# A hybrid decoder layer on one core: other homes for rows and small arrays, row numbers behind up, first weights in three parts

## What is computed

```python
proj = rmsnorm(x) @ w_in                  # 1024 x 7168, eight parts
m = sigmoid(ga) * conv_branch(cv, cg) + sigmoid(gb) * hgrn2_branch(q, f, v, og)
x = x + m @ w_out
# hierarchical experts: top-1 of 4 groups, top-2 of its 8 experts
h = rmsnorm(x)
for e in range(32):
    a = silu(h @ w_expert_gate[e]) * (h @ w_expert_up[e])
    out += combine[:, e:e+1] * (a @ w_expert_down[e])
y = rmsnorm(x + out)                      # and the new states of both branches
```

## Time and profile before

| | us |
|---|---|
| median of 3 runs (802.21 to 802.62) | 802.27 |
| the profiled execution | 801.55 |
| its span | 799.8 |
| TensorE busy | 776.8 |
| mean granted TensorE clock, share of full | 0.996 |
| HBM read | 259.14 MB |

### The profile page before, as it was taken

One profiled execution on the slowest core, in us unless ns is written; L12 is line 12 of the kernel. 1 busy time (PEld: TensorE's weight loads), 2 busy tenths in 40 slices (PEclk: granted clock), 3 DMA queues, 4 the chain that ended last, 5 costly groups with the idle time before them and its releaser, 6 DMA issues.

```text
span 799.8 us, 10083 instructions
## 1 busy us (share of the span) xinstructions
PE 776.8 (97%) x4132; PEld 440.1 (55%) x4132; DVE 236.5 (30%) x540; ACT 172.6 (22%) x313; POOL 96.6 (12%) x130
## 2 busy tenths in 40 slices
PE   8999999999999999999999999999998999999996
PEld 7888888888888887853333333333323333323332
DVE  4099859482550321441201110011101101101102
ACT  3104333657544101410011001110010010011101
POOL 5200064523300000001101000001000000000001
PEclk9999999999999999999999999999999999999999
DMA  9845586668749975589999999999999999999994
GB/s 331 246 153 187 164 236 201 187 211 183 264 147 360 399 265 206 188 325 433 423 429 416 427 429 428 429 425 429 427 426 429 429 427 427 429 426 420 421 410 156
DMA packets 76374, 266.82 MB, mean 334 GB/s; under 512 B 5726, under 2 KB 37706, under 8 KB 63775
## 3 DMA queue, kind: packets, MB, share of 16 engines
q1 hardware_dynamic: 74402, 263.05, 84.4%
q10 hardware_dynamic: 1461, 1.45, 0.6%
q0 software_dynamic: 464, 1.64, 0.5%
HBM read 259.14 MB, written 7.47 MB: 333 GB/s over the span
## 4 chain that ended last, share of the span: by engine, by line
PE 76%; DMA 19%; DVE 1%; issue 1%; POOL 1%; SPq 0%; ACT 0%; DVEq 0%
PE bank L1642 23%; PE bank L2040 22%; DMA slots<-in_w_expert_gate_dram 10%; PE bank L2078 8%; PE bank L1915 7%; PE bank L2086 5%; DMA x_early<-in_w_expert_gate_dram 5%; DMA slot<-in_w_expert_up_dram 3%; PE bank L1862 2%; PE bank L1752 1%; DMA slots<-in_w_in_dram 1%; PE bank L2004 1%; PE bank L1674 1%; PE bank L2067 1%; PE bank L2092 1%
## 5 line engine op out<-in xcount | busy, mean ns | idle before, releaser
L1642 PE MATMUL bank<-hT,slots 128*128 128x264 f32 x832 | 189.6, 387 | 0.0
L2040 PE MATMUL bank<-slots,hT 128*64 128x512 f32 x624 | 181.8, 601 | 5.6 <-DMA slots<-in_w_expert_gate_dram 5.0
L1642 PEld LDWEIGHTS bank<-hT,slots 128*128 128x128 f32 x832 | 156.6, 190 | 26.8 <-issue 0.6
L2040 PEld LDWEIGHTS bank<-slots,hT 128*64 128x64 f32 x624 | 55.8, 138 | 107.3 <-issue 94.2
L1501 DVE TENSOR_TENSOR x_early<-x_early,bank 128x512 f32<-128x512 f32 x16 | 11.0, 688 | 344.5 <-PE bank L2040 344.5
L2078 PE MATMUL bank<-slots,wrep 128*64 128x512 f32 x304 | 85.1, 595 | 0.1
L2040 PE MATMUL bank<-slot,hT 128*64 128x512 f32 x208 | 81.9, 595 | 2.4 <-DMA slot<-in_w_expert_gate_dram 1.7
L2086 PE MATMUL bank<-hT,diag 128*128 128x512 f32 x128 | 64.4, 615 | 0.2 <-ACT hT L1068 0.2
L796 POOL COPY hT<-x_early 128x512 f32 x30 | 17.6, 614 | 369.5 <-PE bank L2040 285.5
L2078 PEld LDWEIGHTS bank<-slots,wrep 128*64 128x64 f32 x304 | 26.1, 137 | 45.6 <-issue 40.1
L1226 DVE SCALAR_TENSOR_TENSOR slot<-slot,rows_buf 128x256 f32<-128x256 f32 x120 | 49.4, 488 | 0.0
(11 more groups left out here) (313 smaller groups left out, 747.7 us busy)
## 6 DMA issues: line engine op xcount, KB each, us to landing
slots<-in_w_expert_gate_dram SPq DMA_DIRECT2D x15, 2048.0 KB, 26.3
slots<-in_w_expert_up_dram SPq DMA_DIRECT2D x15, 2048.0 KB, 31.2
slots<-in_w_expert_down_dram SPq DMA_DIRECT2D x15, 2048.0 KB, 33.6
slots<-in_w_in_dram SPq DMA_DIRECT2D x13, 2048.0 KB, 10.2
slots<-in_w_expert_gate_dram SPq DMA_DIRECT2D x10, 1024.0 KB, 26.4
slot<-in_w_expert_gate_dram SPq DMA_DIRECT2D x5, 2048.0 KB, 25.4
slot<-in_w_expert_up_dram SPq DMA_DIRECT2D x5, 2048.0 KB, 26.2
slot<-in_w_expert_down_dram SPq DMA_DIRECT2D x5, 2048.0 KB, 29.5
```

Of the source, the lines that this page charges most:

```text
L1642: last = mm(out, w[:, a, t * P:(t + 1) * P], (hT if c else xgain)[:, a, :], start=(a == 0), stop=(a == KT - 1))
L2040: last = mm(out[sl, :], xe[:, a, sl], expert_view(p, kind, e, a // 2)[:, a % 2, :], start=(a == 0), stop=(a == KT - 1))
```

## The change

1. *Homes.* The three tiles of `xrow` move: to `ytok` (the upper part of hT), to `rows_buf` and to `early[2D:3D]`. The small arrays move to the place of `act` and to free columns of `xall`. Halves 17 and 19 are free earlier: load 19 is issued ahead of slot 5, load 17 after the squares are summed. The rows are written to memory tile by tile, and ACT waits for that before it writes `ytok` in pair 0.
2. *Row numbers behind up.* `row_numbers` stands behind up(0), the list's copy behind `swiglu(0)` on DVE, and turn(0) waits for it.
3. *First weights in three parts*: 512 KB, 512 KB and 1 MB. The load of `norm_mix_g` moves from SyncE's queue to ACT's, and one of four fillers goes.
4. *Row products of a pair in one block*: all four of `combine_prompt(p - 1)` stand between gate(p) and up(p) (in pair 15 in the middle of gate), and `m_rows` goes.
5. *Whole slots in pair 14*: all its weights come as whole slots and no longer by halves.

```diff
+        small_homes = [act, *(xall[:, a, 2 * P:LISTED] for a in (0, 5, 6, 7))]
+        xrow = [ytok, rows_buf[:, 0:D], early[:, 2 * D:3 * D]]
+        xrow_by = [x.rearrange("p (a q) -> p a q", a=KT) for x in xrow]
...
         def by_halves(p, kind):
-            return p == PAIRS - 2 or (p, kind) in ((1, 2), (PAIRS - 1, 0))
+            return (p, kind) in ((1, 2), (PAIRS - 1, 0))
...
-            sp.dma_start(vecr[0:KT, :], ins["norm_mix_g"][0].rearrange("(r c) -> r c", c=P)).then_inc(gain_in, 16)
...
-            sp.dma_start(slot3(0)[:, 0:KT // 2, :], stream[0][0][:, 0:KT // 2, :]).then_inc(first_in, 16)
+            sp.dma_start(slot3(0)[:, 0:2, :], stream[0][0][:, 0:2, :]).then_inc(first_in, 16)
+            sp.dma_start(slot3(0)[:, 2:KT // 2, :], stream[0][0][:, 2:KT // 2, :]).then_inc(second_in, 16)
...
             load(WO + 1)
+            load_half(NR - 1)
...
             load_half(16)
+            sp.wait_ge(f_sum, KT - 1)
+            load_half(17)
             sp.wait_ge(misc.ready, misc.written(("ht", 5)))
             sp.wait_ge(x_kept, 1)
             load_half(18)
-            sp.wait_ge(row_made, 6)
-            sp.dma_start(tok_rows[0:SEQ, :].rearrange("(t p) d -> p t d", p=P), xrow[:, 0:2, :]).then_inc(rows_kept, 16)
+            for t in range(2):
+                sp.wait_ge(row_made, 2 * t + 4)
+                sp.dma_start(tok_rows[t * P:(t + 1) * P, :], xrow[t]).then_inc(rows_kept, 16)
...
-            sp.wait_ge(rows_kept, 32)
+            load_half(NR)
+            sp.wait_ge(rows_kept, 48)
             sp.wait_ge(m_gathered, 2)
-            load_half(19)
-            sp.wait_ge(smalls_done, 1)
-            load_half(17)
-            load_half(NR)
...
+            se.dma_start(vecr[0:KT, :], ins["norm_mix_g"][0].rearrange("(r c) -> r c", c=P)).then_inc(gain_in, 16)
...
+                if p == 0:
+                    se.wait_ge(rows_kept, 48)
                 if p:
                     se.wait_ge(m_comb, p)
-                    se.wait_ge(m_rows, p)
...
-            dve.wait_ge(m_numbers, 1)
-            dve.tensor_copy(list_at[:, 1:], numbers).then_inc(list_ready, 1)
...
             for p in range(PAIRS):
                 swiglu(p)
+                if p == 0:
+                    dve.wait_ge(m_numbers, 1)
+                    dve.tensor_copy(list_at[:, 1:], numbers).then_inc(list_ready, 1)
...
-            keep_busy(4)
+            keep_busy(3)
...
                 for a in range(4 * half, 4 * half + 4):
+                    if a == 2:
+                        pe.wait_ge(second_in, 16)
...
-                hidden(p, 0, bank[GATE], m_gate, (lambda: combine_prompt(p - 1, 2)) if p == PAIRS - 1 else None)
+                hidden(p, 0, bank[GATE], m_gate, (lambda: combine_prompt(p - 1)) if p == PAIRS - 1 else None)
...
                 else:
-                    pe.wait_ge(smalls_done, 1)
+                    pe.wait_ge(list_ready, 1)
...
                 gate(p)
+                if 1 < p < PAIRS - 1:
+                    combine_prompt(p - 1)
+                up(p)
                 if p == 0:
                     row_numbers()
-                if 1 < p < PAIRS - 1:
-                    combine_prompt(p - 1, 2 if late_rows(p - 1) else 4)
-                up(p)
                 if p:
                     combine_samples(p - 1)
-                if p and late_rows(p - 1):
-                    to_rows(p - 1, 1, 0)
                 turn(p)
-                if p and late_rows(p - 1):
-                    to_rows(p - 1, 1, 1).then_inc(m_rows, 1)
```

More of the change, by code:

```diff
@@ L190, in hybrid_layer @@
         PAIR_ORDER = (1, 0, 2, 3)
-        xrow = early[:, 0:3 * D].rearrange("p (t d) -> p t d", t=3)
-        xrow_by = early[:, 0:3 * D].rearrange("p (t a q) -> p t a q", t=3, a=KT)
         xall = early[:, 3 * D:3 * D + KT * COLS].rearrange("p (a c) -> p a c", a=KT)
@@ L216, in hybrid_layer @@
         wc_zero = dflat[:, T:T + QUART]
-        o = 0
+        taken = [0] * len(small_homes)
         def flat(n):
[L220 to L223, removed]
+            i = next(i for i, home in enumerate(small_homes) if taken[i] + n <= home.shape[1])
+            taken[i] += n
+            return small_homes[i][:, taken[i] - n:taken[i]]
         def small(n):
@@ L276, in hybrid_layer @@
         x_turned, x_gained, x_copied = sem("x_turned"), sem("x_gained"), sem("x_copied")
-        first_in, gain_in = sem("first_in"), sem("gain_in")
+        first_in, second_in, gain_in = sem("first_in"), sem("second_in"), sem("gain_in")
         x_squared, rms_ready, diag_ready = sem("x_squared"), sem("rms_ready"), sem("diag_ready")
@@ L599, in _ @@
             load_half(18)
-            sp.wait_ge(row_made, 6)
-            sp.dma_start(tok_rows[0:SEQ, :].rearrange("(t p) d -> p t d", p=P), xrow[:, 0:2, :]).then_inc(rows_kept, 16)
+            for t in range(2):
+                sp.wait_ge(row_made, 2 * t + 4)
+                sp.dma_start(tok_rows[t * P:(t + 1) * P, :], xrow[t]).then_inc(rows_kept, 16)
             sp.wait_ge(*misc.read(("ht", 5)))
-            sp.dma_start(tok_rows[SEQ:T, :], xrow[0:NB, 2, :]).then_inc(rows_kept, 16)
+            sp.dma_start(tok_rows[SEQ:T, :], xrow[2][0:NB, :]).then_inc(rows_kept, 16)
             sp.wait_ge(quad_ready, 1)
@@ L780, in fetch_rows @@
                 pool.wait_ge(m_gathered, 2 * b)
-                pool.indirect_dma_start(xrow[0:m, 2, :], None, tok_rows[:, :],
+                pool.indirect_dma_start(xrow[2][0:m, :], None, tok_rows[:, :],
                                         bass.IndirectOffsetOnAxis(ap=list_at[0:m, b:b + 1], axis=0)).then_inc(row_in, 16)
@@ L786, in _ @@
             pool.wait_ge(*made("xend"))
-            pool.wait_ge(rows_kept, 32)
+            pool.wait_ge(rows_kept, 48)
             pool.wait_ge(list_ready, 1)
@@ L1033, in _ @@
                 se.wait_ge(y_seated, i + 1)
-                se.activation(xrow_by[:, t, :, SLOTS * half:SLOTS * half + SLOTS],
+                se.activation(xrow_by[t][:, :, SLOTS * half:SLOTS * half + SLOTS],
                               bank[Y_BANKS[t][half]][:, :].rearrange("p (q a) -> p a q", a=KT), ACT.Copy,
@@ L1038, in _ @@
                 se.wait_ge(misc.ready, misc.written(("ht", 4 + half)))
-                se.activation(xrow_by[0:NB, 2, :, SLOTS * half:SLOTS * half + SLOTS],
+                se.activation(xrow_by[2][0:NB, :, SLOTS * half:SLOTS * half + SLOTS],
                               bank[misc.bank(("ht", 4 + half))][0:NB, :].rearrange("p (q a) -> p a q", a=KT), ACT.Copy,
@@ L1488, in _ @@
                 last = dve.tensor_copy(slotpos[lanes, :], spos[lanes, :].rearrange("p (n e) -> p n e", e=2)[:, :, e])
-            last.then_inc(smalls_done, 1)
-            dve.wait_ge(smalls_done, 1)
+            step(last)
             dve.wait_ge(slot_row_ready, 2)
@@ L2003, in first_block @@
                         for c in range(4):
-                            last = mm(bank[GATHER[j]][:, c * P:(c + 1) * P], xrow_by[0:m, t, 4 * j + c, :], sel0[0:m, t, :],
+                            last = mm(bank[GATHER[j]][:, c * P:(c + 1) * P], xrow_by[t][0:m, 4 * j + c, :], sel0[0:m, t, :],
                                       start=(t == 0 and c == 0), stop=(t == 2 and c == 3))
@@ L2026, in gather @@
                     for c in range(4):
-                        last = tr(bank[GATHER[j]][:, c * n:(c + 1) * n], xrow_by[0:n, 2, 4 * j + c, :], ident[0:n, 0:n])
+                        last = tr(bank[GATHER[j]][:, c * n:(c + 1) * n], xrow_by[2][0:n, 4 * j + c, :], ident[0:n, 0:n])
                     last.then_inc(m_gathered, 1)
@@ L2094, in samples_to_rows, with combine_prompt @@
                 return last
-            def combine_prompt(p, parts=4):
+            def combine_prompt(p):
                 pe.wait_ge(m_wc, p + 1)
                 pe.wait_ge(m_ytok, 2 * p + 2)
-                for n in range(parts):
-                    last = to_rows(p, n // 2, n % 2)
-                if parts == 4:
-                    last.then_inc(m_rows, 1)
-            def late_rows(p):
-                return p >= len(BLOCKS) - 2
+                for t in range(2):
+                    for i in range(2):
+                        to_rows(p, t, i)
             def combine_samples(p):
```

3 lines of the change are left out of this document (removed).

## The result

| | before | after |
|---|---|---|
| median of 16 runs, us | 802.41 (801.75 to 803.28) | 805.06 (803.34 to 807.01) |
| ratio, 95% interval | | 1.0032 (1.0025 to 1.0040) |
| the profiled execution | 801.55 | 806.22 |
| its span | 799.8 | 804.5 |
| TensorE busy | 776.8 | 770.6 |

The changed kernel is 2.65 us slower, of its forecast 3.2. The profiled execution lies near the top of its spread. Of the 16 executions, six have a mean granted clock of 0.992 to 0.994 and a median of 806.3 us, ten have 0.995 or 0.996 and a median of 804.0. The mean clock alone does not sort them: two of the ten, 805.38 and 806.66, are as slow as the six.

What follows compares the result with a forecast made beforehand. TensorE's own time was taken to bound the kernel up to 345 us, then the expert weight stream, held by gate(1)'s release. Stream +2.0 and end +1.2 gave +3.2 on 802.27: 805.5 us, range 800.0 to 807.6.

Steps and rivals of the forecast that it cites:

- The fetch and the wait: Before gather(1): indirect fetch issued at 362.9, taking 11.4 us, lands at 374.3; TensorE stands for 3.9 us.
- The clock: After the wait before gather(1): TensorE's clock drops, +1.7 us on gate(1), bounds 0 and 3.4.
- The first rival: At gather(1): the fetch is late but the clock stays; stream +0.4, end +1.6, 803.9 us; chance 0.17.
- The stream: Slots behind gate(1) leave at 387.9, land at 395.7 instead of 393.6; whole weight stream 2.0 us later.
- The fourth rival: Loads 19 and 17 count in full: queue, not gate(1), holds the next slots; 4.9 us back, 798.6; chance 0.04.
- 1.6 us** of queued work: SyncE's queue at 384.19: 9.4 - 7.8 = 1.6 us left, the most that loading 19 and 17 earlier can gain.
- The start: First product of weights starts at 8.25 instead of 9.47: -1.2 us, handed on by TensorE; bounds 0 and -1.5.
- The end: Pairs 14 and 15: whole slots and row products in one block end down(15) at 788.6, not 787.40: +1.2 us.
- The second drop: Ahead of gate(14): a wait of 2.6 us drops the clock again, +1.7 us more, 807.2; chance 0.17.

Runs made afterwards that it cites:

- `b3`: Kernel before plus new homes, first weights in three parts, one filler less and the gains on ACT's queue: 800.04 us, ratio 0.9976.
- the fillers' run: Changed kernel plus seven filler products between down(0) and gather(1): 804.51 us, ratio 1.0029.
- `b4`: `b3` plus gate weights of pair 1 and down weights of pair 2 loaded by halves: 799.06 us, ratio 0.9962.

## Why the prediction was right, and where not

Forecast 805.5 (800.0 to 807.6), slower with 0.63; measured 805.06, +2.65 over before where the sum had +3.2. Direction, cause and order of events were right. That the median came within 0.5 us is in part luck: it lies between two kinds of execution, which the forecast did not know of, and the sum missed the profiled one by 1.4 us, on two terms. The runs split this into three parts, each against before of its own session: homes and start -2.0 (`b3`), the end +1.8 (row numbers in front again against `b3`), the row numbers behind up(0) +2.8. Step by step:

- **The fetch and the wait.** Issue 362.9 forecast, 362.69 measured; latency 11.4 and 11.40; landing 374.3 and 374.09; a wait of 3.9 and 3.9. The choice of 11.4 between 9.0 and 11.9, since whole slots stand in the other queue, is borne out by the run with halves, where it was 9.1. It was not certain: in the fillers' run the same fetch took 8.9 among whole slots.
- **The clock.** The term "**+1.7** on gate(1)" rested on one drop of 3.4 us and is mis-sized: in the profiled execution TensorE was at the lower level for 6.8 us, and gather(1) and the row products took 1.97 + 5.00 where they take 1.09 + 3.67, 2.2 us more. In other executions the clock fell for 3.4 us ahead of the wait, where the fetch covers it. The prediction took the clock as one case of one size, and it is two. The first rival, "*the wait without the clock*", 803.9, has the time of the milder one, but not its mechanism: there too the clock falls.
- **The stream.** Slots issued at 388.20 and landed at 396.0; forecast 387.9 and 395.7. That the release behind gate(1) is the bound, read from 9.4 against 7.8 us, holds: an earlier gate(1) moves the landing and the time, and so does a finer release. The fourth rival falls. But "**1.6 us** of queued work", the number that was to decide, is too large by 0.9 us, and this is the largest term that failed. It compared the landing of the first slot only, and the gap closes behind it: the first slot behind the release needs 9.4 us before and 7.8 in after, the second gate slot of pair 3, the fourth load, 18.1 and 17.4. So that slot lands at 412.9 where it was 409.6, and the stream is 3.3 us late, not 2.4 as at 396.0 and not 2.0 as forecast. Nor is it slowed on the way: from 396 to 412 the DMA share is 1.02 at 432 GB/s in after and 1.00 at 424 before. The same 0.7 us, added to the change in the release time, gives the fourth load in other profiles with the new homes: homes alone 0.2 - 0.7 = -0.5 (measured -0.4), the milder execution of after 1.9 - 0.7 = +1.2 (+1.1), the end as before 4.8 - 0.7 = +4.1 (+4.0). Why a landing tells less than the whole stream was not tried. That the two early loads gain 0.8 us and not 1.6 fits it.
- **The start.** "**-1.2 us**, and TensorE hands it on": mis-sized. The first product starts at 8.24, as forecast, and gate(0) at 344.07, 1.2 before the 345.28 of before. But over the twelve profiles of kernels with this start gate(0) begins between 344.07 and 345.46, on average at 344.8, and the start alone gained 0.6 us, in an interval that reaches nothing; in its one profile the fourth load lands at 410.3, 0.8 later than before. What differs are the transposes of x ahead of the first product, in after and then in its execution with the milder drop (timeline: start, us, engine, line, operation):

```profile
5.58 2.64 PE L1602 MATMUL bank<-ident,slots 128*128 128x128 f32 x16
8.24 2.02 PE L1755 MATMUL bank<-x_early,slots 128*128 128x264 f32 x8
```
```profile
5.58 3.62 PE L1602 MATMUL bank<-ident,slots 128*128 128x128 f32 x16
8.99 1.37 PE L1755 MATMUL bank<-x_early,slots 128*128 128x264 f32 x5
```

  The same 16 products take 2.64 us in one and 3.62 in the other; weights are not late in either. The clock comes up later. The windows print 1.00 from the start, but the trace's own record of the clock begins, at the upper level, only at 7.07 us in after and at 9.17 in the other. In the twelve profiles the 16 products take 2.64, 2.72, 3.17, 3.30 and 3.52 us where this record begins at 7.07, 7.23, 8.12, 8.41 and 8.84, and 3.62 us in the seven where it begins later.
- **The end.** "**+1.2**": 1.1 to 1.8, by several comparisons. Gate(14) is started by weights, down(15) by no wait, as forecast, and from one to the end of the other TensorE takes 53.80 us where the sum had 27.0 + 26.76. But gate(14) starts at 738.20 where 734.83 + 2.0 = 736.8 was forecast: of these 1.4 us 1.3 are the stream's, 3.3 late and not 2.0.
- **Open.** What makes the clock fall early in one execution and late in another, and why the fetch's neighbour queue ran short in the fillers' run and not in the others, was not tried.
- **The second drop**, third rival: not in the profiles of after, though one wait of 2.4 us stands there, at 647.7.

## What to carry to other kernels

Before work is moved back on the busiest engine, ask what other queues wait for its result: twelve small products worth 3.6 us, moved behind 7 us of work, delayed an indirect fetch, the fetch a release, and the release every later load. A stream that looks 100% busy is bound by a release where the load behind it lands as fast as on an empty queue; then loading other things earlier gains only what is left in the queue, and cutting the loads behind the late release finer gains more. Size what is left by a load several places behind the release: the first landing said 1.6 us, the fourth 0.7, and the time agreed with the fourth. And where the times of one kernel fall into two groups, a forecast needs a size for each, and a profile of each to explain them.

## What the hardware showed that I had not expected

- The clock fell without a long wait. In three profiles (the milder one of after, the fillers, the gate weights by halves) it was down for 3.4 us from 363.4 to 365.1 on, behind the 12 small products and around `turn(0)`, where no gap was over 0.7 us. With the row numbers ahead of up(0) it stayed up there in all profiles.
- After the wait of 3.9 us it was down for 6.8 us, of which TensorE worked 5.0; after the wait of 2.0 us in the earlier trace rows for 3.4. In `b4` a wait of 1.9 us at 641.8 was followed by a drop of 3.4 us at 644.4, while a wait of 2.4 us at 647.7 in after and of 2.7 in `b3` were followed by none: the length of a wait did not decide it.
- Which of the two drops comes seems settled in the first 10 us. In the six profiles with the row numbers behind up, those with the late, long drop have their first product of weights at 8.24, 8.32 and 8.57, those with the early, short one at 8.71, 8.98 and 8.99. By the record of the clock it came up at 7.07, 7.23 and 8.12 us in the first three, and fell 365.2 us later in each; in the other three it came up at 8.41, 9.17 and 10.13, and fell 355.0 us later in each. Six profiles show an order, not a cause.
- An indirect fetch of 128 rows took 10.1 to 11.9 us among pieces of 16 KB, with the one exception of 8.9 in the fillers' run; 8.8 to 9.8 when it was issued behind pieces of 8 KB; and 5.4 to 7.1 when it was issued between 378.0 and 378.9, as the other queue ran dry.
